# Steps of an attention stage spread over more rounds, with a gate's projection beside them; earlier copies of projections and a norm end in two parts

## The chip, the cores and the metric

The kernel runs on one core of a Trainium2 chip. The metric is the device time of one execution in microseconds (us); the time before is the median of three runs. The engines are TensorE (PE in the profile; PEld is its loading of weights), VectorE (DVE), ScalarE (ACT), GpSimd (POOL) and SyncE (SP), which here only starts transfers.

## The reference, cut to what matters

Three blocks follow one another on 512 tokens of width 1024, all in float32. The change touches two places.

The first is the even mixer of block one. Its input projection gives, among others, the queries, keys and values of a delta rule, a gate `z` (512 columns) that only scales the delta rule's output, and the queries, keys and values of a differential attention:

```python
qkv_a, z_a, b_a, a_a, q_b, k_b, v_b = split_cols(h @ w_in, EVEN_SPLITS)
o_a = gated_delta_rule(q_a, k_a, v_a, g, beta)
o_a = rms_norm(o_a, gdn_norm_w) * silu(z_a)
# differential attention: 4 heads, 4 blocks of 128 queries, causal
a = softmax(s0) - lam * softmax(s1)        # two score maps per head
o_b = a @ v_b
```

The second is the RWKV part of block three: eight pairs of heads run a delta rule with a per-channel decay over chunks of 64 tokens. Its inputs r, k, v are projections mixed with the token before (`out = (1-m)*t + m*shift(t)`), and its output goes through a group norm of 64 channels, gets a bonus term added and is multiplied by a gate `g` (a small matmul):

```python
y = group_norm(o) * gn_g + gn_b + bonus
y = y * g
```

## The kernel before, in words

Every engine has its own program, written out by Python; semaphores (`wait_ge`) join them. Activations are feature-major: a tile is 128 channels x 512 tokens. A projection (`Weights.tile`) of 128 output channels is 24 matmuls of 128x512: eight slices of the contraction, each in three products of a high and a low fp32r part. The weights come by SP's transfers into three raw buffers (two neighbouring tiles in one 1 MB transfer); ACT makes the high part (L87) and DVE the low part (L96), one tile ahead of the matmuls. `Weights.half` gives half a tile, 12 matmuls, and holds its PSUM bank in between. `Psum.take` hands out the eight banks in turn; before a bank is written again, PE waits for the engine that reads it out.

**Even mixer.** `Even.pe` orders the projections: 12 tiles `even.qkv`, 4 tiles `even.z`, one of 8 columns `even.ba`, 8 tiles `even.rope` with a rotation matmul each, then `even.dv`. When `even.ba` is done ACT copies it and then starts the transfer of the positions; from these DVE and ACT make the sine and cosine tables, and the copy of the first rope tile stands behind them on ACT. `z` goes through Silu as it is copied from PSUM. A fence of all engines follows, then the differential attention (`diff_*`), a fence, and the delta rule (`gdn_*`).

The attention has 16 units (head, query block `qt`). `waves(16, 4)` gives every engine the order: in round r the unit r-3 does its phase 3, unit r-2 phase 2, unit r-1 phase 1, unit r phase 0. Phase 0: PE makes two score maps (`diff.s`). Phase 1: DVE takes the masked maximum of each (L105), ACT the exponential with its sum (L84). Phase 2: DVE takes reciprocals (L108), scales and joins the two maps (L99, L102), PE transposes the result block by block (L93), and DVE (even units) or ACT (odd ones) copies it out (L87). Phase 3: PE multiplies with the values, and the other of the two engines copies the 128x128 result. Within phase 2 all of this is one chain.

**RWKV.** `Rwkv.steps` gives the orders. There are 16 units u (a pair of heads n = u//2, half of the tokens each), one started every six rounds; a unit's steps stand in the list `order`, one a round. Within a round an engine goes through the kinds of step in its own tuple (`PE`, `ACT`, `DVE`, `POOL`). Beside these run the projections of r, k, v of the next pair (kind `proj`, rounds 4 to 9 of each twelve, half a tile a round) and a convolution (`cf`: projections in rounds 0 to 3; `tap`: products on ACT, sums on POOL, and taps on DVE). When a second half is done ACT copies the projection twice (`shift_act`: into a padded buffer, L87, and scaled, L83), and that frees its bank; in `ACT` this stands behind the kinds `p` and `g`. Of kind `p`, step `pB` on ACT is a square root that waits for a matmul of the same round, a table load, and an exponential that waits for a scan on DVE (L3195). The group norm is `gn1` to `gn3`, an empty round, and `gn4`: there PE spreads the reciprocal roots (16 matmul instructions of 128x128 and 64 columns of weights) and makes the gate's matmul, and DVE does three operations of 128x512. ACT's next `out` waits for the last of them (`rw_gn`).

## Time and profile before

| | |
|---|---|
| median of three runs | 3913.9 us (3910.14 to 3914.62) |
| profiled execution | 3902.29 us, its span 3899.7 us |
| PE, DVE, ACT, POOL busy | 88%, 52%, 33%, 9% of the span |
| granted clock of TensorE, mean | 0.93 |
| matmuls of 128x512 fp32r | 10368, 2468.5 us busy |

Times are in us from the start of the span. A row of windows has the stretch, its length, then the busy time (and instructions) of PE, PEld, DVE, ACT and POOL, then PEclk, the DMA share and GB/s. In a timeline a row is a run of like instructions: start, duration, engine, line, operation, output and inputs, count, and in brackets the idle time before it and what ended it. PEclk is the granted clock as a share of 2.4 GHz, so that 0.50 is 1.2 GHz. Only the part up to 460 us (even mixer) and that from 2550 to 3250 us (RWKV) are touched.

### The profile page before, as it was taken

Reading aid. Unit: us, or ns where it says so; the run is one execution under the profiler, and the core shown is the slowest. Engines: PE = TensorE matmul, PEld = TensorE weight load, DVE = VectorE, ACT = ScalarE, POOL = GpSimd, SP = SyncE. Lnnn points to the kernel's source line nnn. Section 1 sums busy time; section 2 is a strip of 40 time slices with the busy share of each in tenths; the row PEclk is TensorE's granted clock in tenths of the full one; section 3 lists DMA queues with packets and bytes.
Section 4 is the critical chain, followed back from the end, with each engine's and each line's share of the span. In section 5 each row is a group of like instructions: output and inputs, shape, how many; then the busy total and the mean of one; then the engine's idle time right before and its main releaser. Section 6 shows DMA issues by size and latency. Waiting matters only on the chain.

```text
span 3899.7 us, 50586 instructions
## 1 busy us (share of the span) xinstructions
PE 3445.0 (88%) x20778; PEld 2657.7 (68%) x20778; DVE 2039.2 (52%) x3588; ACT 1295.9 (33%) x2133; POOL 366.1 (9%) x338
## 2 busy tenths in 40 slices
PE   6876889999799999998797889878989889998998
PEld 4645867777586677776666666456777777777886
DVE  5435446664422456654454435468676773445443
ACT  3222133222222332223333234355454542324221
POOL 0001200000000000000001000035443430000000
PEclk8976989999898999999897989889899989999999
DMA  3210013442343134432211120021111102232221
GB/s 132 66 43 1 1 60 108 135 141 87 60 88 74 33 92 130 137 107 87 79 52 42 47 80 12 27 87 45 32 38 41 48 13 76 71 114 86 91 94 64
DMA packets 318851, 274.89 MB, mean 70 GB/s; under 512 B 10912, under 2 KB 310048, under 8 KB 317856
## 3 DMA queue, kind: packets, MB, share of 16 engines
q1 hardware_dynamic: 314368, 256.07, 22.3%
q10 hardware_dynamic: 4256, 15.59, 1.1%
q8 instruction: 167, 2.74, 0.3%
q14 instruction: 60, 0.49, 0.0%
HBM read 265.35 MB, written 6.29 MB: 70 GB/s over the span
## 4 chain that ended last, share of the span: by engine, by line
PE 75%; DVE 14%; ACT 5%; issue 3%; DMA 1%; POOL 1%; DVEq 0%; ACTq 0%; SPq 0%; POOLq 0%
PE ps L90 73%; DVE f L102 5%; DVE f L96 3%; DVE r L96 3%; PE ps L93 2%; ACT f L83 2%; DVE f L99 2%; DVE f L108 1%; ACT r L87 1%; ACT f L87 1%; POOL f L96 1%; ACT L83 1%; ACT f L84 1%; DVE f L3195 0%; DVE f L105 0%
## 5 line engine op out<-in xcount | busy, mean ns | idle before, releaser
L90 PE MATMUL ps<-r,r 128*128 128x512 f32 x10368 | 2468.5, 397 | 143.5 <-DVE r L96 99.3
L90 PEld LDWEIGHTS ps<-r,r 128*128 128x128 f32 x10368 | 1931.9, 191 | 632.4 <-issue 193.6
L90 PE MATMUL ps<-f,f 64*64 64x64 f32 (+10 forms) x9458 | 909.0, 283 | 234.1 <-DVE f L96 58.9
L90 PEld LDWEIGHTS ps<-f,f 64*64 64x64 f32 (+4 forms) x9458 | 641.8, 162 | 485.3 <-issue 256.5
L96 DVE TENSOR_TENSOR r<-f,r 128x1024 fp32r<-128x1024 f32 (+2 forms) x619 | 654.3, 1063 | 491.7 <-ACT r L87 484.8
L87 ACT ACTIVATE r<-f 128x1024 fp32r<-128x1024 f32 (+2 forms) x548 | 507.1, 938 | 824.6 <-PE ps L90 679.7
L87 ACT ACTIVATE f<-ps 128x512 f32<-128x512 f32 (+3 forms) x414 | 184.6, 460 | 669.5 <-PE ps L90 424.7
L102 DVE SCALAR_TENSOR_TENSOR f<-f,f,f 128x128 f32<-128x128 f32 (+3 forms) x622 | 362.0, 588 | 41.6 <-ACT f L83 25.5
L96 POOL TENSOR_TENSOR f<-f,f 128x512 f32<-128x512 f32 (+2 forms) x280 | 322.1, 1164 | 514.5 <-ACT f L83 293.7
L96 DVE TENSOR_TENSOR f<-ps,f 128x512 f32<-128x512 f32 (+4 forms) x325 | 178.1, 561 | 327.7 <-PE ps L90 320.1
L83 ACT ACTIVATE f<-ps 128x512 f32<-128x512 f32 (+3 forms) x203 | 111.9, 553 | 636.3 <-PE ps L90 634.5
L96 DVE TENSOR_TENSOR f<-f,f 128x256 f32<-128x256 f32 (+5 forms) x372 | 220.8, 605 | 18.7 <-ACT f L83 10.1
L96 POOL TENSOR_TENSOR r<-f,r 128x512 fp32r<-128x512 f32 (+1 forms) x25 | 38.5, 1539 | 1985.4 <-ACT r L87 1985.4
L96 DVE TENSOR_TENSOR f<-f 128x512 f32<-128x512 f32 x129 | 86.9, 687 | 227.8 <-ACT f L83 216.5
L108 DVE RECIPROCAL f<-f 128x1 f32<-128x1 f32 (+4 forms) x193 | 72.3, 382 | 212.7 <-ACT f L84 106.1
L93 PE MATMUL ps<-f,f 128*128 128x128 f32 (+2 forms) x568 | 110.9, 316 | 63.3 <-DVE f L102 29.3
L83 ACT ACTIVATE f<-f 128x512 f32<-128x512 f32 (+8 forms) x206 | 100.3, 514 | 187.7 <-DVE f L102 86.1
L96 DVE TENSOR_TENSOR f<-f,ps 128x512 f32<-128x512 f32 (+1 forms) x192 | 110.7, 593 | 73.3 <-PE ps L90 62.7
L93 PEld LDWEIGHTS ps<-f,f 128*128 128x128 f32 (+2 forms) x568 | 73.4, 159 | 90.3 <-DVE f L102 34.0
L83 ACT ACT_TABLE_LOAD x90 | 115.5, 1283 | 32.1 <-DVE f L105 19.0
L83 ACT ACTIVATE f<-f,f 128x512 f32<-128x512 f32 (+2 forms) x165 | 109.5, 705 | 14.9 <-POOL f L96 13.9
L102 DVE SCALAR_TENSOR_TENSOR f<-ps,f,f 128x512 f32<-128x512 f32 x48 | 36.0, 751 | 146.2 <-PE ps L90 141.5
(32 smaller groups left out, 733.4 us busy)
## 6 DMA issues: line engine op xcount, KB each, us to landing
f<-in_w_mlp_up SPq DMA_DIRECT2D x32, 1024.0 KB, 6.5
f<-in_w_mlp_down SPq DMA_DIRECT2D x32, 1024.0 KB, 6.5
f<-in_w_ff SPq DMA_DIRECT2D x32, 1024.0 KB, 5.3
f<-in_w_ada SPq DMA_DIRECT2D x48, 512.0 KB, 4.1
f<-in_w_in SPq DMA_DIRECT2D x24, 1024.0 KB, 5.3
f<-in_w_in SPq DMA_DIRECT2D x44, 512.0 KB, 3.8
f<-in_w_in_even SPq DMA_DIRECT2D x12, 1024.0 KB, 6.0
f<-in_w_in_odd SPq DMA_DIRECT2D x12, 1024.0 KB, 13.1
```

Of the source, the lines that this page charges most:

```text
L83: return self.e.activation(out, in_, func, bias=bias, scale=scale)
L84: return self.e.activation(out, in_, func, bias=bias, scale=scale, accum_out=acc)
L87: return self.e.activation(out, in_, ACT.Copy) if self.name == "act" else self.e.tensor_copy(out, in_)
L90: return self.e.matmul(out, l, r, start=first, stop=last)
L93: return self.e.transpose(out, in_, ident)
L96: return self.e.tensor_tensor(out, a, b, op)
L99: return self.e.tensor_scalar(out, a, s1, None, o0) if o1 is None else self.e.tensor_scalar(out, a, s1, s2, o0, o1)
L102: return self.e.scalar_tensor_tensor(out=out, in0=a, scalar=s, in1=b, op0=o0, op1=o1)
L108: return self.e.reciprocal(out, in_)
```

## The change

In the even mixer the four tiles of `z` leave the projections. They become eight half tiles, one at the start of each of the attention's first eight rounds; ACT copies each finished tile without Silu, and four Silu of 128x512 stand behind the last round, before the fence. The unit's steps get a round each: transposes are phase 3, the product with the values phase 4, its copy phase 5. All copies of transposes go to ACT; the products of a head's four blocks gather in one held bank, copied once by ACT. DVE has maxima and the joining of the maps only, the maxima first in a round. In RWKV, ACT's kinds `cf` and `proj` are split: the steps of odd rounds (second halves, with their copies) come before `p` and `g`. The group norm's end is two steps: `gn4` (PE's spread and DVE's scaling) goes into the empty round, a round earlier, and `gn5` (the gate's matmul, the other two operations) stays.

```diff
@@ Even.pe
-        for n in range(4):
-            G.tile(pe, ("even.z", n), W, 1536 + n * 128, 128, X, [("ev_z", n + 1)])
@@ Even.diff_pe
-        for u, p in waves(16, 4):
+        K, G, X = self.K, self.K.G, self.norm.X
+        for u, p in waves(16, 6):
             if p == 0:
+                if u < 8:
+                    G.half(pe, ("even.z", u // 2), self.W, 1536 + u // 2 * 128, X, [("ev_z", u // 2 + 1)], u % 2)
                 for m in range(2):
...
-            elif p == 2:
+            elif p == 3:
                 pe.wait_ge("diff_a", u + 1)
-                b = self.bank["t", u] = K.ps.take(pe, ("diff_pt" + "da"[u % 2], u // 2 + 1))
+                b = self.bank["t", u] = K.ps.take(pe, ("diff_pt", u + 1))
...
-            elif p == 3:
-                pe.wait_ge("diff_pt" + "da"[u % 2], u // 2 + 1)
-                b = self.bank["o", u] = K.ps.take(pe, ("diff_o" + "ad"[u % 2], u // 2 + 1))
+            elif p == 4:
+                pe.wait_ge("diff_pt", u + 1)
+                if qt == 0:
+                    self.bank["o", h] = K.ps.hold(pe, ("diff_o", h + 1))
+                b = self.bank["o", h]
                 for kt in range(qt + 1):
...
@@ Even.act
-        for n in range(4):
-            G.act(act, ("even.z", n))
-            act.wait_ge("mm", K.done["even.z", n])
-            act.f(self.z[:, n, :], G.at["even.z", n], ACT.Silu).then_inc(S("ev_z"), 1)
@@ Even.diff_act
-        for u, p in waves(16, 4):
+        for u, p in waves(16, 6):
-            if p == 1:
+            if p == 0 and u < 8:
+                k = ("even.z", u // 2)
+                self.K.G.act(act, k)
+                if u % 2:
+                    act.wait_ge("mm", K.done[k])
+                    act.cp(self.z[:, u // 2, :], self.K.G.at[k]).then_inc(S("ev_z"), 1)
+            elif p == 1:
...
-            elif p == 2 and u % 2:
+            elif p == 3:
                 act.wait_ge("mm", K.done["diff.t", u])
...
-            elif p == 3 and not u % 2:
+            elif p == 5 and qt == 3:
                 act.wait_ge("mm", K.done["diff.o", u])
-                act.cp(self.o[:, 4 + h, qt * 128:km], K.ps.t[self.bank["o", u]][:, 0:128]).then_inc(S("diff_oa"), 1)
+                act.wait_ge("mm", K.done["even.z", 3])
+                act.cp(self.o[:, 4 + h, :], K.ps.t[self.bank["o", h]][:, :]).then_inc(S("diff_o"), 1)
+        act.wait_ge("ev_z", 4)
+        for n in range(4):
+            act.f(self.z[:, n, :], self.z[:, n, :], ACT.Silu).then_inc(S("ev_zs"), 1)
@@ Even.diff_dve
-        for u, p in waves(16, 4):
+        for u, p in ((r - p, p) for r in range(21) for p in (1, 2, 0) if 0 <= r - p < 16):
+            if p == 0 and u < 8:
+                K.G.dve(dve, ("even.z", u // 2))
-                if not u % 2:
-                    dve.wait_ge("mm", K.done["diff.t", u])
...
-                    dve.cp(self.pt[u % 3][:, 0:km], K.ps.t[self.bank["t", u]][:, 0:km]).then_inc(S("diff_ptd"), 1)
-            elif p == 3 and u % 2:
-                dve.wait_ge("mm", K.done["diff.o", u])
-                dve.cp(self.o[:, 4 + h, qt * 128:km], K.ps.t[self.bank["o", u]][:, 0:128]).then_inc(S("diff_od"), 1)
@@ Rwkv
-    ACT = ("out", "xy", "tm", "fin", "p", "g", "cf", "proj", "tap")
+    ACT = ("out", "xy", "tm", "fin", "cf1", "proj1", "p", "g", "cf", "proj", "tap")
@@ Rwkv.steps
-        order += ["fin", ("c", 0), ("c", 1), ("c", 2), ("c", 3), "out", "gn1", "gn2", "gn3", "", "gn4"]
+        order += ["fin", ("c", 0), ("c", 1), ("c", 2), ("c", 3), "out", "gn1", "gn2", "gn3", "gn4", "gn5"]
...
-                elif k == "proj":
-                    if r < 84 and 4 <= r % 12 < 10:
+                elif k in ("proj", "proj1"):
+                    if r < 84 and 4 <= r % 12 < 10 and (not split or r % 2 == (k == "proj1")):
@@ Rwkv.pe, after the spread of gn4
+            elif p == "gn5":
                 pe.wait_ge("rw_xg", 1)
                 b = self.bank["g3", n] = take(pe, ("rw_gn", n + 1))
                 K.mm_done(pe.mm(P[b][:, :], self.g2[:, ncol], self.xg, True, True), ("rw.g3", n))
@@ Rwkv.dve, after gn4's scaling by gn_g
+            elif p == "gn5":
                 dve.wait_ge("rw_ys", n + 1)
```

## Rows read from the trace of the kernel before

**Rows 1.** Windows: even projections, attention, and four RWKV periods; columns as told above.

```profile
37.00:266.60 229.60, 197.95 (x748) 138.77 (x748) 106.03 (x145) 64.01 (x87) 0.00 (x0) 0.92 0.22 66
266.60:350.30 83.70, 52.51 (x184) 31.07 (x184) 39.53 (x166) 25.29 (x82) 0.00 (x0) 0.56 0.00 0
2837.50:3168.00 330.50, 287.81 (x4151) 234.07 (x4148) 235.46 (x446) 163.46 (x294) 135.98 (x126) 0.92 0.13 38
```

**Rows 2.** Waits in the window 264:372 (us in total, times, longest).

```profile
ACT f L84 <- DVE f L105: 36.8, 9, 5.4
...
PE ps L93 <- DVE f L102: 29.3, 16, 3.4
```

**Rows 3.** Timeline of all engines, attention: table load, then a unit with `qt` 3.

```profile
267.48 1.28 ACT L83 ACT_TABLE_LOAD   x1 [18.97 <-DVE f L105]
268.77 0.20 ACT L83 ACTIVATE f<-f 128x2 f32<-128x2 f32 x1
...
281.95 0.68 DVE L105 CUSTOM_DVE_ANT_0 f<-ps,f 128x512 f32<-128x512 f32 x1
...
290.07 0.29 DVE L87 COPY f<-ps 128x128 f32<-128x128 f32 x1 [3.77 <-PE ps L90]
...
310.14 0.29 DVE L87 COPY f<-ps 128x128 f32<-128x128 f32 x1 [3.95 <-PE ps L90]
```

**Rows 4.** Timeline of PE alone, one RWKV period.

```profile
2947.81 0.68 PE L90 MATMUL ps<-f,f 64*64 64x64 f32 x16 [0.73 <-ACT f L83]
...
2956.10 2.02 PE L90 MATMUL ps<-f,f 64*64 64x64 f32 x32 [2.11 <-ACT f L83]
2958.06 5.00 PE L90 MATMUL ps<-r,r 128*128 128x512 f32 x12
...
2977.41 1.12 PE L90 MATMUL ps<-f,f 64*64 64x64 f32 x16 [3.86 <-issue]
2980.16 1.99 PE L90 MATMUL ps<-f,f 64*64 64x128 f32 x32 [1.62 <-issue]
...
3000.53 1.20 PE L90 MATMUL ps<-f,f 64*64 64x64 f32 x32 [1.21 <-ACT f L87]
3001.66 3.01 PE L90 MATMUL ps<-r,r 128*128 128x512 f32 x12
```

**Rows 5.** Timeline of PE alone, even projections.

```profile
38.05 13.92 PE L90 MATMUL ps<-r,r 128*128 128x512 f32 x48 [16.65 <-DVE r L96]
53.06 11.32 PE L90 MATMUL ps<-r,r 128*128 128x512 f32 x48 [1.10 <-DVE r L96]
...
114.27 33.23 PE L90 MATMUL ps<-r,r 128*128 128x512 f32 x144 [0.88 <-DVE r L96]
156.32 2.08 PE L90 MATMUL ps<-f,f 128*128 128x512 f32 x2 [8.83 <-ACT f L87]
```

**Rows 6.** The page's groups: DVE's part of the weight splits, among others.

```profile
L96 DVE TENSOR_TENSOR r<-f,r 128x1024 fp32r<-128x1024 f32 (+2 forms) x619 | 654.3, 1063 | 491.7 <-ACT r L87 484.8
```

**Rows 7.** Timeline of ACT alone, seventh round of that period.

```profile
2952.67 0.17 ACT L83 ACTIVATE f<-ps 128x4 f32<-128x4 f32 x1 [2.29 <-PE ps L90]
...
2955.37 0.68 ACT L83 ACTIVATE f<-ps,f 128x512 f32<-128x512 f32 x1
```

**Rows 8.** Windows: 3 us behind the gap that ends at 2956.10.

```profile
2956.00:2959.00 3.00, 2.90 (x34) 2.66 (x35) 2.44 (x6) 3.00 (x7) 2.12 (x2) 0.50 0.00 0
```

**Rows 9.** Timeline of PE alone: behind the same wait in another period, and a spread.

```profile
3042.36 3.92 PE L90 MATMUL ps<-r,r 128*128 128x512 f32 x12
...
3245.28 1.97 PE L90 MATMUL ps<-f,f 128*64 128x128 f32 x16 [0.59 <-DVE f L108]
```

**Rows 10.** Timeline of DVE alone, third, eighth and ninth round.

```profile
2927.11 1.22 DVE L96 TENSOR_TENSOR f<-f,f 128x256 f32<-128x256 f32 x3
...
2963.48 0.28 DVE L102 SCALAR_TENSOR_TENSOR f<-f,f,ps 128x64 f32<-128x64 f32 x1 [3.49 <-PE ps L90]
...
2969.98 3.24 DVE L96 TENSOR_TENSOR f<-f,f 128x256 f32<-128x256 f32 x3
2973.15 0.73 DVE L102 SCALAR_TENSOR_TENSOR f<-f,f,ps 128x512 f32<-128x512 f32 x1
```

More of the change, by code:

```diff
@@ L17 @@
 STAGES = (
-    {"ev_z": 4, "ev_pad": 12, "ev_padz": 3, "ev_conv": 12, "ev_qkv": 12, "ev_bar": 1, "ev_ba": 1, "ev_y": 1, "ev_na": 1,
-     "ev_beta": 1, "ev_rope": 8, "ev_dv": 4},
-    {"diff_elam": 1, "diff_exp": 32, "diff_oa": 8, "diff_pta": 8, "diff_lam": 2, "diff_max": 32, "diff_a": 16, "diff_ptd": 8,
-     "diff_od": 8},
+    {"ev_pad": 12, "ev_padz": 3, "ev_conv": 12, "ev_qkv": 12, "ev_bar": 1, "ev_ba": 1, "ev_y": 1, "ev_na": 1, "ev_beta": 1,
+     "ev_rope": 8, "ev_dv": 4},
+    {"diff_elam": 1, "diff_exp": 32, "ev_z": 4, "diff_pt": 16, "diff_o": 4, "ev_zs": 4, "diff_lam": 2, "diff_max": 32,
+     "diff_a": 16},
     {"gdn_expR": 4, "gdn_DTe": 4, "gdn_ekdf": 4, "gdn_ebE": 4, "gdn_y0": 12, "gdn_y1": 12, "gdn_NW": 4, "gdn_o": 4,
@@ L1006, in diff_pe @@
                 K.mm_done(t, ("diff.t", u))
-            elif p == 3:
-                pe.wait_ge("diff_pt" + "da"[u % 2], u // 2 + 1)
-                b = self.bank["o", u] = K.ps.take(pe, ("diff_o" + "ad"[u % 2], u // 2 + 1))
+            elif p == 4:
[3 more added lines that the diff above has]
+                b = self.bank["o", h]
                 for kt in range(qt + 1):
-                    t = pe.mm(K.ps.t[b][:, 0:128], self.dv[:, kt, h * 128:h * 128 + 128], self.pt[u % 3][:, kt * 128:kt * 128 + 128],
-                              kt == 0, kt == qt)
+                    t = pe.mm(K.ps.t[b][:, qs], self.dv[:, kt, h * 128:h * 128 + 128], self.pt[u % 3][:, kt * 128:kt * 128 + 128],
+                              qt + kt == 0, qt + kt == 6)
                 K.mm_done(t, ("diff.o", u))
+                if qt == 3:
+                    K.ps.leave(b)
     def gdn_pe(self, pe):
@@ L1148, in diff_act @@
                     act.wait_ge("mm", K.done["diff.o", u - 3])
-                act.cp(self.pt[u % 3][:, 0:km], K.ps.t[self.bank["t", u]][:, 0:km]).then_inc(S("diff_pta"), 1)
-            elif p == 3 and not u % 2:
+                act.cp(self.pt[u % 3][:, 0:km], K.ps.t[self.bank["t", u]][:, 0:km]).then_inc(S("diff_pt"), 1)
+            elif p == 5 and qt == 3:
                 act.wait_ge("mm", K.done["diff.o", u])
-                act.cp(self.o[:, 4 + h, qt * 128:km], K.ps.t[self.bank["o", u]][:, 0:128]).then_inc(S("diff_oa"), 1)
+                act.wait_ge("mm", K.done["even.z", 3])
[3 more added lines that the diff above has]
+            act.f(self.z[:, n, :], self.z[:, n, :], ACT.Silu).then_inc(S("ev_zs"), 1)
     def gdn_act(self, act):
@@ L1194, in dve @@
             t.then_inc(S("ev_conv"), 1)
-        for n in range(4):
-            G.dve(dve, ("even.z", n))
         G.dve(dve, "even.ba")
@@ L2875, in steps @@
         order = ["pA", "pB", "pC", "pD", "pE", "tm", "i0"] + [(k, l) for l in range(1, 6) for k in "yx"]
-        order += ["fin", ("c", 0), ("c", 1), ("c", 2), ("c", 3), "out", "gn1", "gn2", "gn3", "", "gn4"]
-        kind = {"x": "xy", "y": "xy", "gn1": "g", "gn2": "g", "gn3": "g", "gn4": "g"}
+        order += ["fin", ("c", 0), ("c", 1), ("c", 2), ("c", 3), "out", "gn1", "gn2", "gn3", "gn4", "gn5"]
+        kind = {"x": "xy", "y": "xy", "gn1": "g", "gn2": "g", "gn3": "g", "gn4": "g", "gn5": "g"}
+        split = "proj1" in kinds
         kind.update((k, "p") for k in order[0:5])
@@ L2886, in steps @@
             for k in kinds:
-                if k in ("cf", "tap"):
+                if k in ("cf", "cf1", "tap"):
                     for m, what, q in self.cf.steps(r - behind if k == "tap" else r):
-                        if (k == "tap") == (what in ("tap", "keep")):
+                        if (k == "tap") == (what in ("tap", "keep")) and (k == "tap" or not split or q == (k == "cf1")):
                             yield m, m, 0, "cf" + what, q
-                elif k == "proj":
-                    if r < 84 and 4 <= r % 12 < 10:
+                elif k in ("proj", "proj1"):
+                    if r < 84 and 4 <= r % 12 < 10 and (not split or r % 2 == (k == "proj1")):
                         n = r // 12 + 1
```

5 lines of the change are left out of this document (1 added, 4 removed).

## The prediction

> **What bounds the kernel now.** I read first the windows by stage. While the even projections run, PE is busy 198 of 230 us at a clock of 0.92, so whatever PE does there costs its full time; in the attention it is busy 52.5 of 83.7 us at 0.56, DVE 39.5 and ACT 25.3 [rows 1]. No engine is full there. The waits tell the rest: ACT stands 36.8 us for DVE's maxima and PE 29.3 us for DVE's joined maps [rows 2], a chain of one unit after another. In the timeline the same copy comes back after 20.07 us (290.07, 310.14) [rows 3]: four units take that, 5.02 each. In RWKV PE is busy 288 of 330 us, DVE 235, ACT 163, at 0.92 [rows 1]. That is near PE's limit, and what can be won is PE's idle time and what the low clock behind it costs. A period (twelve rounds, one pair of heads, a fourth of that window: 82.6 us) has five such gaps: 0.73, 2.11, 3.86, 1.62 and 1.21 us [rows 4].
>
> **Part 1a: `z` leaves the projections.** 144 matmuls (z, ba, the first rope tile) run without a break in 33.23 us [rows 5]; 96 of them are z: 22.2 us. Behind them PE waits 8.83 us for the first rope copy [rows 5]. That wait hangs on `even.ba` (copy, transfer of the positions, tables), and moves with it; nothing on it gets shorter. But ba's small weights are ready sooner than a full tile's, so of the gap of 0.88 us at 114.27 [rows 5] most goes too. Removed: 23.0 us (bounds 22.2 and 23.1). z's four Silu copies on ACT lay under PE's matmuls, so leaving them out is worth nothing there.
>
> **Part 1b: the attention.** I take the new stage in four pieces.
> Rounds 0 to 7: z's 96 matmuls, 22.2 us on PE. A start at the low clock costs 13.92 - 11.32 = 2.6 us more [rows 5]. Beside it PE has 8 units' scores, 5 of transposes and 4 of products, about 1.35 heads of the 4. The stage's 52.5 us at 0.56 [rows 1] are 52.5 x 0.56 / 4 = 7.35 us a head at full clock, so 9.9. Sum 34.7, or 4.3 a round. What else runs is hidden under that: DVE's 39.5 us [rows 1] less its sixteen copies (about 5.7) are 2.1 a unit, and a weight split of some 1.1 [rows 6] every second round; ACT has less. The first unit's wait for lambda goes under z as well. The two 1 MB weight transfers move behind those of `even.dv`, on SP's queue alone; the DMA share in this stage is 0.00 [rows 1], so they are hidden, and `even.out`'s, now behind them, are needed only after the delta rule. If not hidden, the first would be late by a few us.
> Rounds 8 to 15: every step now stands a round from the next. DVE's 2.1 us a unit are 2.4 with gaps; PE has 52.5 / 16 = 3.3 at about the low clock, 1.8 at the full. Which of them holds depends on the clock, so I take 2.7, nearer DVE, the engine that the waits name: 21.6 (bounds 19.2 and 26.4).
> Drain of the last unit: as now from the first maximum to the last copy, 281.95 to 290.36, 8.4 us [rows 3].
> The four Silu at the end are covered by nothing, since the fence waits for them: a table load of 1.28 us [rows 3] and four times 0.6, the present copies' time, 3.7 us.
> Sum 68.4 against 83.7: 15.3 saved. The delta rule's first Exp now needs a table load too, in front of work that DVE waits for: 1.3 lost (0 if it runs while PE is still at work).
> The Trainium skill (ScalarE: Activation LUTs, "What ACT_TABLE_LOAD costs") speaks against this edit: it puts each switch of table set at about 2.66 us, drain included. In the trace the load is 1.28 us and the activation behind it starts 0.01 us later [rows 3]; by the Trainium skill's figure the two switches would cost 5.3 us in place of 2.6, and the saving would be 2.7 less.
> Part 1: 23.0 + 15.3 - 1.3 = 37.0 us (bounds 31 and 40).
>
> **Part 2: RWKV.** Following `take` and `hold` through a period shows whose bank PE waits for.
> (a) In the eighth round the second `x` step takes the bank of the projection whose copies stand behind ACT's `pB`. ACT's root waits 2.29 us for PE until 2952.67; the scaled copy begins only at 2955.37 [rows 7], and when it ends PE resumes, at 2956.10 [rows 4]. Put in front, both copies (1.2 us) fit into the 2.29 and delay the root by nothing or little. PE gets back 2.1 us, and more: behind the gap the clock is 0.50 [rows 8], the twelve matmuls take 5.00 us in place of 3.01, the 32 small ones 2.02 in place of 1.20 [rows 4]. That makes 4.9 us in three periods and 3.6 in two (3.92 in place of 3.01 [rows 9], the small ones in proportion), and 3.4 in an earlier one: 25.3. Against it, PE's spread of `gn4` now stands before the end of this round: 1.97 us at the low clock [rows 9], 1.0 at the full, five times. Net 20.3.
> (b) In the second round it is the convolution's bank: 1.21 us [rows 4], five times, 6.0.
> (c) The 0.73 us of the seventh round [rows 4] wait for the norm's root behind DVE's shifted sum, which is late by ACT's copy; I take half, as PE's own matmul then comes last: 2.0 in all.
> (d) The 3.86 us [rows 4] wait for DVE, which in the ninth and tenth round does product, norm end, shift and `x` without a pause. One of these, 0.73 us [rows 10], moves a round forward, where DVE stands idle for 3.49 us [rows 10]: 3.7 in five periods. The 1.62 us behind it stay.
> Sum 32.0. Against this, POOL's masks stand behind the convolution's sums, and PE will now ask for them some 3 us sooner; I take off 6.0, a little over 1 us a period, as an estimate without a row. Part 2: 26 us (bounds 0 and 36).
>
> **Sum.** 63 us. The profiled execution took 3902.3 us, 2.6 of them around its span, and would take 3839.3; the median of the runs shown is 11.6 us above it, so I predict 3913.9 - 63 = 3851 us.
>
> **Rivals.**
> R1: the freed bank only shows the next wait. DVE's ninth round and POOL's masks set the period, and RWKV gives 8 in place of 26: 3869. For it: DVE has 235 of 330 us of work [rows 1], and the longest gap is already its own. Against: DVE itself waits 3.49 us for PE in the eighth round [rows 10].
> R2: the clock stays low in the attention. z's matmuls take twice their time, 22 us more: 3873. For it: the stage is at 0.56 now [rows 1]. Against: the same matmuls one behind the other lose only 2.6 us at a cold start [rows 5].
> R3, the other side: DVE's operations on two SBUF operands are slower beside POOL's sums; three of 128x256 take 3.24 us in one round and 1.22 in another [rows 10], 0.67 us more for each. If the closer packing brings 19 more of them a period under POOL, a period grows by 12.7 us and five of them by 63, and from there on the kernel is slower; with 25 it takes 3935. For it: that row. Against: POOL is busy 136 of 330 us [rows 1], and the overlap can as well shrink.
> The Trainium skill (SBUF — State Buffer, "Who interferes with whom") has this as a lock: such an operation and one of GpSimd that reads SBUF exclude each other. By that rule the trace agrees, as 1.08 us for an operation of 0.41 is a wait and not a slower rate alone.
>
> **How the numbers follow.** Chances: forecast 0.66, R1 0.16, R2 0.11, R3 0.03, no gain in either part 0.04. What a measurement of this kernel can tell from no change is 0.2%, 7.8 us. The forecast's own range is 3838 (both parts at their upper bounds) to 3864; with R1 and R2 and a little of both together it is 3835 to 3881. From the same cases: faster 0.93, same 0.04, slower 0.03.
>
> **What would show it.** Right: no z between qkv and ba, and the attention starting 23 us sooner; the attention in 66 to 72 us, with the clock near 1 in its first half, DVE almost without waits in its second, and a table load with four activations behind the last copy; in RWKV no PE wait of 2.1 or 1.2 us on L83 or L87, the full clock in the eighth round, a period of 77 to 78 us. Wrong: z halves of 5 us, rounds over 5 us, or a new PE wait on POOL or DVE in rounds eight to eleven.

## The result and the profile after

| | before | after |
|---|---|---|
| timed runs, median | 3912.1 us (3910.1 to 3914.6, 4 runs) | 3821.7 us (3820.8 to 3823.2, 4 runs) |
| profiled execution, span | 3899.7 us | 3819.4 us |
| mean granted clock of PE | 0.930 | 0.943 |

The ratio of the runs is 0.9769, with a 95% interval of 0.9752 to 0.9786: the kernel is 2.3% faster. Forecast were 3851 us and a range of 3835 to 3881, so the direction was right and the time is 13 us below the range. The gain is 90.4 us by the medians and 80.3 us by the two traces; 63 were forecast.

GpSimd's memsets mark the borders of stages. These are the rows of after, from the timeline of POOL alone: the first is the start of the delta rule, the second the stage behind it, `128x1` the start of the RWKV blocks, and each `128x64` one pair of heads.

```profile
307.20 0.52 POOL L114 MEMSET f<- 128x512 f32 x1 [269.56 <-ACTq L76]
1010.93 2.30 POOL L114 MEMSET f<- 128x160 f32 x5
2509.94 0.25 POOL L114 MEMSET f<- 128x1 f32 x4 [72.55 <-DMA x_rest<-f]
...
3128.26 0.15 POOL L114 MEMSET f<- 128x64 f32 x1
```

In before the same rows stand at 350.48, 1053.64, 2552.38 and 3207.96. So after is 43.3 us ahead at the delta rule, 42.4 at the start of the RWKV blocks and 79.7 at their end. Two places gave everything: what lies ahead of the delta rule, and the RWKV blocks (655.6 us before, 618.3 after: 37.3).

The windows of after, which answer to [rows 1]: even projections, attention, and two RWKV periods.

```profile
core 0: us, PE busy (x) PEld busy (x) DVE busy (x) ACT busy (x) POOL busy (x), PEclk, DMA share, GB/s
37.00:243.70 206.70, 175.25 (x652) 120.29 (x652) 101.94 (x141) 58.55 (x80) 0.64 (x4) 0.91 0.21 63
243.70:307.20 63.50, 54.01 (x280) 37.23 (x281) 38.87 (x154) 37.66 (x99) 0.00 (x0) 0.96 0.11 34
2861.84:2938.88 77.04, 71.23 (x1039) 57.83 (x1036) 60.72 (x112) 41.71 (x75) 35.78 (x32) 0.93 0.13 39
2938.88:3015.51 76.63, 70.46 (x1038) 57.15 (x1036) 60.67 (x112) 41.57 (x75) 35.71 (x32) 0.96 0.13 40
```

In the attention PE now carries 96 more matmuls and is busy for nearly the same time as before, 54.0 against 52.5 us, because its clock is 0.96 and no longer 0.56. The stage is 63.5 us long instead of 83.7. A finer cut shows its two halves, with z and without:

```profile
243.70:278.86 35.16, 35.11 (x163) 24.86 (x163) 18.68 (x69) 17.82 (x44) 0.00 (x0) 0.95 0.19 61
278.86:296.20 17.34, 15.08 (x93) 9.40 (x92) 16.53 (x73) 12.70 (x42) 0.00 (x0) 1.00 0.00 1
281.20:289.84 8.64, 7.51 (x46) 4.70 (x46) 8.23 (x37) 6.45 (x21) 0.00 (x0) 1.00 0.00 1
```

With z, PE is busy 35.1 of 35.2 us: it is the bound. Without z a round takes 8.64 / 4 = 2.16 us, and DVE (8.23 of 8.64) is the fullest engine, PE (7.51) close behind. The end of the stage, from the last copy on, and the delta rule's load, on ACT alone:

```profile
302.87 0.60 ACT L87 ACTIVATE f<-ps 128x512 f32<-128x512 f32 x1 [1.25 <-PE ps L90]
303.48 1.28 ACT L83 ACT_TABLE_LOAD   x1
304.78 2.19 ACT L83 ACTIVATE f<-f 128x512 f32<-128x512 f32 x4
309.78 1.28 ACT L83 ACT_TABLE_LOAD   x1 [2.82 <-PE ps L90]
```

In RWKV, PE's waits from the first marker to the last, first of before (655.6 us), then of after (618.3 us); columns: total, times, longest.

```profile
PE ps L90 <- issue: 45.7, 19, 8.1
PE ps L90 <- ACT f L83: 20.6, 12, 4.7
...
PE ps L90 <- ACT f L87: 6.5, 6, 1.2
```

```profile
PE ps L90 <- issue: 44.5, 18, 7.2
...
PE ps L90 <- ACT f L83: 4.7, 1, 4.7
PE ps L90 <- ACT f L87: 2.1, 5, 0.7
```

What PE waited for on ACT went from 27.1 to 6.8 us, 20.3 us; nothing else moved by more than 1.2. PE's busy time fell too, with the same 7651 matmuls, from 564.1 to 548.3 us: 15.7 us, which I put down to the low clock behind those waits (it is 548.4 us too where ACT's order alone is changed, below). 20.3 + 15.7 + 1.3 make the 37.3. The timeline of PE in a period of after, beside [rows 4]:

```profile
2971.17 3.02 PE L90 MATMUL ps<-r,r 128*128 128x512 f32 x12
...
2977.11 3.06 PE L90 MATMUL ps<-r,r 128*128 128x512 f32 x12
...
2988.64 1.12 PE L90 MATMUL ps<-f,f 64*64 64x64 f32 x16 [3.94 <-issue]
2991.38 1.98 PE L90 MATMUL ps<-f,f 64*64 64x128 f32 x32 [1.62 <-issue]
...
2996.37 1.40 PE L90 MATMUL ps<-f,f 64*64 64x64 f32 x40 [0.36 <-ACT f L87]
```

The twelve matmuls of the eighth round take 3.02 us in place of 5.00, and of the period's five gaps two are left, those behind DVE, of the same size as before. One wait behind ACT's L87 remains, of 0.36 us.

### The profile page after: what moved, and what is told of

Its sections match the earlier page's. It is cut to its first block, busy times and chain, and to the rows that moved or that the text cites. A ratio compares the mean times of both kernels' runs of the same rounds, so it can differ in the third digit from the quotient of the medians.

```text
span 3819.4 us, 50585 instructions
## 1 busy us (share of the span) xinstructions
PE 3408.5 (89%) x20778; PEld 2633.2 (69%) x20778; DVE 2047.8 (54%) x3572; ACT 1304.7 (34%) x2143; POOL 374.7 (10%) x338
## 4 chain that ended last, share of the span: by engine, by line
PE 77%; DVE 12%; ACT 5%; issue 3%; DMA 1%; POOL 1%; DVEq 0%; ACTq 0%; SPq 0%; POOLq 0%
PE ps L90 75%; DVE f L102 4%; DVE f L96 3%; DVE r L96 3%; PE ps L93 2%; ACT f L83 2%; DVE f L108 1%; DVE f L99 1%; ACT r L87 1%; ACT L83 1%; POOL f L96 1%; ACT f L87 1%; DVE f L105 0%; ACT f L84 0%; DMA f<-in_w_in_odd 0%
## 5 line engine op out<-in xcount | busy, mean ns | idle before, releaser
L90 PE MATMUL ps<-f,f 64*64 64x64 f32 (+11 forms) x9458 | 885.9, 278 | 215.3 <-DVE f L96 59.0
L90 PEld LDWEIGHTS ps<-f,f 64*64 64x64 f32 (+4 forms) x9458 | 626.5, 159 | 458.5 <-issue 254.8
L87 ACT ACTIVATE r<-f 128x1024 fp32r<-128x1024 f32 (+2 forms) x548 | 507.1, 938 | 825.7 <-PE ps L90 681.0
L87 ACT ACTIVATE f<-ps 128x512 f32<-128x512 f32 (+3 forms) x422 | 189.5, 465 | 668.7 <-PE ps L90 416.6
L96 POOL TENSOR_TENSOR f<-f,f 128x512 f32<-128x512 f32 (+2 forms) x280 | 330.7, 1194 | 469.7 <-ACT f L83 256.9
L93 PE MATMUL ps<-f,f 128*128 128x128 f32 (+2 forms) x568 | 106.5, 307 | 36.7 <-DVE f L99 19.0
```

The lines of the kernel that those rows point to most:

```text
L87: return self.e.activation(out, in_, ACT.Copy) if self.name == "act" else self.e.tensor_copy(out, in_)
L90: return self.e.matmul(out, l, r, start=first, stop=last)
L93: return self.e.transpose(out, in_, ident)
L96: return self.e.tensor_tensor(out, a, b, op)
```

## The experiments

Four columns are taken from the memsets of each trace: the time to the start of the delta rule; the delta rule (from there to the `128x160` memset); and the RWKV blocks (`128x1` to the last `128x64`). What lies between is 1498 to 1502 us in all traces but one. Medians of different experiments compare only roughly: the kernel after itself gave 3821.7 us in one session and 3833.3 in another. So what an edit is worth is read below from the stages of the traces.

| kernel | timed median, us | ratio to before [95%] | to delta rule | delta rule | RWKV |
|---|---|---|---|---|---|
| before | 3912.1 | 1 | 350.5 | 703.2 | 655.6 |
| after | 3821.7 | 0.9769 [0.9752, 0.9786] | 307.2 | 703.7 | 618.3 |
| attention only | 3866.4 | 0.9898 [0.9878, 0.9918] | 307.0 | 704.0 | 655.6 |
| RWKV only | 3871.6 | 0.9912 [0.9897, 0.9927] | 353.6 | 706.6 | 619.9 |
| ACT's order only | 3869.6 | 0.9907 [0.9892, 0.9922] | 351.6 | 707.0 | 619.6 |
| norm split only | 3908.3 | 1.0003 [0.9993, 1.0013] | 352.4 | 707.6 | 655.8 |
| z back | 3831.2 | 0.9805 [0.9791, 0.9820] | 311.6 | 705.2 | 618.4 |
| Silu later | 3820.7 | 0.9782 [0.9766, 0.9798] | 303.3 | 704.1 | 618.3 |
| sums moved | 3828.6 | 0.9793 [0.9771, 0.9816] | 309.8 | 709.4 | 614.4 |
| both of these | 3818.9 | 0.9774 [0.9759, 0.9788] | 307.0 | 705.2 | 614.3 |
| steps adjacent | 3847.1 | 0.9845 [0.9831, 0.9860] | 326.1 | 708.4 | 618.3 |
| projections first | 3883.2 | 0.9935 [0.9919, 0.9952] | 351.6 | 708.1 | 627.9 |
| convolution first | 3890.9 | 0.9959 [0.9944, 0.9974] | 350.9 | 703.2 | 642.3 |
| both, first block as it was | 3817.9 | 0.9771 [0.9757, 0.9784] | 303.8 | 703.8 | 617.2 |
| after again | 3833.3 | 0.9812 [0.9798, 0.9825] | 308.3 | 704.1 | 621.0 |
| before again | 3908.0, one run | | 352.5 | 707.5 | 655.5 |

Each ratio is against runs of before on the same chip; their medians were 3905.7 to 3907.8 us in these experiments.

**The two parts apart.** Each part alone, put into the kernel before. For the attention:

```diff
+        for u, p in waves(16, 6):
+            if p == 0 and u < 8: G.half(pe, ("even.z", u // 2), ...)
...
     ACT = ("out", "xy", "tm", "fin", "p", "g", "cf", "proj", "tap")    # as before
```

> The kernel before with the whole first part (z's projections inside the attention, its steps a round apart, one bank of outputs for a head, Silu behind it) and none of the changes to the RWKV blocks. My theory: the two parts do not meet, so this gives what the marker at the start of the delta rule moved between the two traces, 43.3 us, less the 0.8 us that the delta rule gave back: about -42.5 us, 0.989 of the time before. The attention stretch takes 63 to 64 us against 83.7. Rival A: part of the 90 us is a shift of the whole program (the median of before stood 10 us above its profiled execution, the median of after did not), so this kernel's timed runs gain 10 us more than its trace shows. Rival B: the RWKV blocks lose clock or place when they start earlier: less than 38 us are gained.

Measured: -41.4 us by the medians, -43.0 by the spans (3856.7). The attention's window is the same as in after, 63.5 us at a clock of 0.96.

> The kernel before with all changes to the RWKV blocks' order (early copies on ScalarE, the norm's end in two steps) and none to the attention. My theory: 37.9 us, as the stretch of the RWKV blocks shrank between the two traces, 0.990 of the time before; this and the run with the attention's part alone add up to the whole change within 2 us by their traces. Rival: the 10 us between the profiled execution and the timed runs of before belong to one of the two parts; then one of these two kernels gains 48 to 53 us in its timed runs.

Measured: -36.2 us by the medians; the RWKV blocks shrink by 35.7 us. The medians of the two add up to 77.6 us, the stages of the two traces to 43.5 + 35.7 = 79.2, beside 80.3 for the whole. So the parts add up, and neither hides 10 us. The trace of the second kernel has one surprise: the stages ahead of RWKV, whose code is that of before, are 6.8 us longer than in the trace of before. That is taken up below.

**Which edit of the RWKV part does it.**

```diff
-    ACT = ("out", "xy", "tm", "fin", "p", "g", "cf", "proj", "tap")
+    ACT = ("out", "xy", "tm", "fin", "cf1", "proj1", "p", "g", "cf", "proj", "tap")
```

> The kernel before with ScalarE's new order alone: its copies of projections and convolution results for a pair's odd rounds go ahead of the steps p and g; the norm's end is not split. My theory: PE's waits for a bank in the eighth round (12 gaps of about 5 us in the trace of before, one in each pair) and the low clock behind them are ScalarE's lateness, so this alone gives most of the 37.9 us: the gap of 5.00 goes and the clock stays at its upper level in the eighth round, 2.1 us of each pair, and with it the 0.73 and 2.1 gaps ahead of it: -24 us or so, 20 to 30. Rival: the 5 us gap is set by VectorE's gn4 step behind it as much as by ScalarE (both free the same bank's neighbours), and the order alone gives under 12 us.

The other edit alone:

```diff
-        order += [..., "gn1", "gn2", "gn3", "", "gn4"]
+        order += [..., "gn1", "gn2", "gn3", "gn4", "gn5"]
...
+            elif p == "gn5":
```

> The kernel before with the norm's end split alone: gs and its product in one round, g3 and what follows it one round later; ScalarE's order is as before. My theory: PE does not wait for gs and g3 of one round together, but its bank waits in the eighth round stay, since ScalarE still copies late: between 3 and 14 us faster (the 37.9 us less what the order alone gives). Rival: splitting alone makes the pipeline one round deeper with nothing gained where ScalarE is late: within 3 us of before, or slower.

ACT's order alone brings RWKV to 619.6 us, as far as both edits together (619.9): 36.0 us, over the 20 to 30 that I expected. That expectation also misread a row: the 5.00 us of [rows 4] are the duration of twelve matmuls at the low clock and no gap, and the wait ahead of them is the 2.11. The split of the norm's end alone leaves RWKV at 655.8. It is worth nothing in either company. The eighth round, in the timeline of PE, of the kernel with the split alone:

```profile
2962.28 2.02 PE L90 MATMUL ps<-f,f 64*64 64x64 f32 x32 [2.09 <-ACT f L83]
2964.23 4.94 PE L90 MATMUL ps<-r,r 128*128 128x512 f32 x12
...
2983.58 1.12 PE L90 MATMUL ps<-f,f 64*64 64x64 f32 x16 [3.94 <-issue]
```

and with ACT's order alone:

```profile
3024.27 3.02 PE L90 MATMUL ps<-r,r 128*128 128x512 f32 x12
...
3027.99 2.16 PE L90 MATMUL ps<-f,f 64*64 64x64 f32 x36 [0.45 <-DVE f L102]
...
3036.86 1.12 PE L90 MATMUL ps<-f,f 64*64 64x64 f32 x16 [3.43 <-issue]
```

With the split the gap behind DVE is 3.94 us, without it 0.45 + 3.43. The DVE work that the split takes forward returns its wait elsewhere. The other half of my expectation, 3 to 14 us from the split, was wrong.

**Which copies of ACT.** ACT's new order cut in two: only the projections' copies first, or only the convolution's.

```diff
-    ACT = (..., "fin", "p", "g", "cf", "proj", "tap")
+    ACT = (..., "fin", "proj1", "p", "g", "cf", "proj", "tap")     # one kernel
+    ACT = (..., "fin", "cf1", "p", "g", "cf", "proj", "tap")       # the other
```

> The kernel before with only one half of ScalarE's new order: its copies of the projections' odd rounds (5, 7 and 9 of a pair's twelve) go ahead of the steps p and g, those of the convolution's inputs stay behind. My theory: TensorE's wait of 5 us and the lower clock in the eighth round, and the 2.1 us gap ahead of it, are for banks that projection copies free; this half gives most of the order's 36 to 38 us, 25 to 35. Rival: the convolution's copies (rounds 1 and 3) are the late ones, and this half gives under 10 us.

> The kernel before with only the other half: ScalarE's copies of the convolution's inputs in rounds 1 and 3 of a pair go ahead of p and g, the projections' copies stay behind. My theory: this half gives the rest, 2 to 10 us (the gap of 1.21 us in the first rounds of a pair, and what it hides). Rival: it gives over 20 us.

RWKV shrinks by 27.7 us with the projections' copies first and by 13.3 with the convolution's first; 36.0 with both. In the timeline of PE of the second, the eighth round's wait is still there, but the clock behind it is back sooner:

```profile
2950.96 1.20 PE L90 MATMUL ps<-f,f 64*64 64x64 f32 x32 [2.07 <-ACT f L83]
2952.08 4.62 PE L90 MATMUL ps<-r,r 128*128 128x512 f32 x12
```

The 32 small matmuls take 1.20 us where before took 2.02 [rows 4], at the same wait ahead of them. In this period that is 0.8 us, and 0.4 at the twelve behind them, 1.2 beside the 1.21 of the gap that goes. The convolution's half was over my 2 to 10 us. The two halves alone add up to 41.0 us and give 36.0 together, so they share 5.0. Most of that is clock: PE's busy time in RWKV falls by 12.4 us with the one, by 6.7 with the other and by 15.7 with both.

**What distance and z do in the attention.** The steps of a unit next to each other again, in the kernel after:

```diff
-        for u, p in waves(16, 6):
+        for u, p in waves(16, 4):
...
-            elif p == 3:        # transpose; ACT's copy of it likewise
+            elif p == 2:
-            elif p == 4:        # product
+            elif p == 3:
...
-        for u, p in ((r - p, p) for r in range(21) for p in (1, 2, 0) if 0 <= r - p < 16):
+        for u, p in ((r - p, p) for r in range(19) for p in (2, 1, 0) if 0 <= r - p < 16):
```

> The kernel after with the attention's steps for a unit put back next to each other: TensorE transposes two rounds behind the scores and multiplies three rounds behind (not three and four), ScalarE copies the transposed tile in the same round as TensorE makes it, and VectorE takes its steps in the old order. One bank of outputs for a head, ScalarE doing all copies and z inside stay. My theory: a round again holds a chain VectorE, TensorE, ScalarE, TensorE of one unit, which in the trace of before made a round of 4 to 5 us out of engines that have 2 to 3 us of work; the eight rounds with z hide part of it (+0.5 us each), the eight without go from 2.2 to about 4 us: 15 to 20 us slower than after, with the lower clock of TensorE (0.56 in before) coming back in the second half. Rival: the gain comes from ScalarE doing all copies and from the output bank held for a head (fewer copies, fewer waits for a bank), and distance adds little: under 6 us slower.

Measured: the attention takes 18.9 us longer. (The delta rule takes 4.6 us longer too, but a kernel with the attention of after, the one with the sums moved, has 709.4 us there, so that this is not shown to come from the steps.) The window of the attention, and then one wait in the part without z, from the timeline of PE:

```profile
243.70:326.05 82.35, 62.94 (x280) 42.08 (x280) 39.38 (x152) 37.67 (x99) 0.00 (x1) 0.83 0.08 26
```

```profile
287.93 1.12 PE L93 MATMUL ps<-f,f 128*128 128x128 f32 x4 [2.16 <-DVE f L102]
```

PE waits for DVE's joined maps as before, and the stage's clock falls from 0.96 to 0.83, so that the same 280 matmuls keep PE busy for 62.9 us and not 54.0. So the distance between the steps is worth much, and the rival's "under 6 us" is wrong. The edit moves the steps of PE and of ACT and DVE's order within a round at once; which of the three counts for how much was not separated. The stage is nearly as long as the old one, 82.4 and 83.7 us, but with z's matmuls in it, and so distance is not all. In the half without z, DVE's joining of a full map, in the timeline of DVE alone:

```profile
302.06 0.75 DVE L102 SCALAR_TENSOR_TENSOR f<-f,f,f 128x512 f32<-128x512 f32 x1
316.99 0.75 DVE L102 SCALAR_TENSOR_TENSOR f<-f,f,f 128x512 f32<-128x512 f32 x1
```

Four units take 14.9 us here, 20.1 in before [rows 3] and 8.6 in after: 3.7, 5.0 and 2.2 each. Of the 2.9 us a unit gained, distance gives 1.6. The other 1.3 come with what this kernel shares with after: ACT's copies, the held bank and the higher clock that z's half leaves behind (0.79 from 278.8 to 318.0 us, 0.56 in the old stage). Which of them is not shown.

z's projections and their Silu back where they were, with the new steps:

```diff
+        for n in range(4):
+            G.tile(pe, ("even.z", n), W, 1536 + n * 128, 128, X, [("ev_z", n + 1)])
...
-                if u < 8:
-                    G.half(pe, ("even.z", u // 2), ...)
```

> The kernel after with z's four projections and their Silu back among the even projections; the attention keeps its new steps, a round apart. My theory: the two edits of the first part are worth about 22.9 us (z out of the projections) against its price inside the attention. Back in the projections z costs 22.9 us again; the attention's first eight rounds fall from 4.3 to the 2.2 us of the rounds without z (about -17 us), and Silu with its table load leaves the end (-3.5 us), and the delta rule's table load goes (-1.3 us). So +1 to +3 us against after: moving z is worth next to nothing in itself, and the new steps alone carry the 42 us. Rival A: TensorE works through the attention at its upper clock because z's matmuls fill it; without them the clock falls back to its lower level in the attention (0.56 in the trace of before) and in the delta rule behind it, and the kernel is 10 to 20 us slower than after. Rival B: z's rounds are longer than 2.2 us by less than z's work, and the kernel is over 5 us slower than after with the clock high.

Measured in the trace: 5.8 us more than after where RWKV starts. The attention is 45.0 us long, at a clock of 0.77:

```profile
266.60:311.60 45.00, 36.94 (x184) 23.46 (x183) 33.63 (x150) 27.63 (x86) 0.00 (x0) 0.77 0.00 1
```

z costs 22.9 us in the projections and 18.5 us in the attention, its Silu included: 4.4 us of gain. Another 1.5 us lie in the delta rule, which is within what its length varies by (below). My +1 to +3 us were too low. Rival A had the mechanism, the clock does fall, but not its 10 to 20 us; Rival B had the size and not its high clock. So of the 42.4 us that after is ahead at the start of RWKV, 36.7 are there without moving z.

Of the 43.3 us by which the delta rule starts sooner, the distance accounts for 18.9 (the run before this one) and moving z for 4.4, each taken out of the full kernel. The 20.0 that remain belong to no edit that was isolated. Either ACT's copies and the held bank are worth that (sixteen times the 1.3 us above are 21, an estimate), or distance and z are worth more apart than on top of each other, since both use the idle time that PE had in the old attention, 31.2 of 83.7 us [rows 1]. Before with the new copies and the held bank alone was not run.

**The work at the attention's end.** The four Silu go into rounds of the delta rule's last chunk:

```diff
-        act.wait_ge("ev_z", 4)
-        for n in range(4):
-            act.f(self.z[:, n, :], self.z[:, n, :], ACT.Silu).then_inc(S("ev_zs"), 1)
...
+                if c == 3 and p in (4, 6, 8, 10):
+                    z = self.z[:, p // 2 - 2, :]
+                    act.f(z, z, ACT.Silu).then_inc(S("ev_zs"), 1)
```

> The kernel after with the four Silu of z moved from the attention's end into rounds of the delta rule's last chunk, where ScalarE is idle. My theory: behind the attention's last copy everything waits for ScalarE: a table load of 1.28 us, four Silu of 2.19 us, and the delta rule's first Exp loads its table again, 1.28 us; all three leave the path, 3.5 + 1.3 = 4.8 us, and the loads come back in the last chunk, where up to 2.6 us of them could show if ScalarE is needed there. So -3 to -5 us against after. Rival: the delta rule's start is held by PE and VectorE work that goes on beside these, and nothing is gained (within 1 us).

The delta rule starts 3.9 us sooner, 3.6 to 4.0 us are kept at the later markers, and 3.2 by the spans. Of the 3.9, 0.4 lie ahead of the attention's last copy. From the start of that copy to the start of the delta rule it is 4.33 us in after and 0.83 here: 3.5 us, which is the four Silu (2.19 us) and the table load (1.28 us). All three traces with this edit have 0.83 or 0.84 us there. In the kernel with both edits the delta rule nevertheless starts at 307.0 us: its attention starts 0.8 us later than that of after, and the clock is 0.65 in its last 11 us and not 0.91. The Trainium skill (ScalarE: Activation LUTs, "What ACT_TABLE_LOAD costs") puts a switch at about 2.66 us, which would make it 4.9 us for the switch and the four Silu, an estimate; the trace does not agree, neither with its 3.5 us nor with the rows at 303.48 and 309.78 above, where each load is 1.28 us. What the second load, inside the delta rule, costs is not seen: that stage takes 704.1 us without it and 703.7 with it.

**DVE beside GpSimd.** GpSimd's sums leave the ninth and tenth round and follow two steps later:

```diff
     def products(self, t):
-        return range(2 * t, min(2 * t + 2, self.more))
+        s = t if t < 3 else t - 2
+        return range(2 * s, min(2 * s + 2, self.more)) if t not in (3, 4) else range(0)
```

> The kernel after with the sums that GpSimd adds up in an RWKV pair taken out of the two rounds in which VectorE has its long operations (3.25 us each, three in a row, beside GpSimd's five of 8.19 us) and put one or two rounds later. My theory: VectorE's operations are stretched by GpSimd's while both work on SBUF (the same form takes 1.22 us elsewhere), and VectorE is what the one long gap of PE left in a period waits for (3.94 us, in the tenth round): the three operations fall to about 1.2 us and the gap with them, 3 to 4 us in each of five to six pairs, -15 to -20 us. Rival: GpSimd then stretches other work of VectorE in the rounds that it moves to by as much, and the time is within 3 us of after or above it.

> Both at once: Silu in the delta rule's last chunk and GpSimd's sums in later rounds. My theory: they touch different stages and add up, -18 to -25 us against after. Rival: as for each of them alone; then it is no better than the better one of the two.

The tenth round in after, DVE, then POOL:

```profile
2981.99 3.25 DVE L96 TENSOR_TENSOR f<-f,f 128x256 f32<-128x256 f32 x3
```

```profile
2982.06 2.88 POOL L96 TENSOR_TENSOR f<-f,f 128x512 f32<-128x512 f32 x2 [1.90 <-ACT f L83]
```

and the same with both edits, DVE, then PE:

```profile
2979.13 1.22 DVE L96 TENSOR_TENSOR f<-f,f 128x256 f32<-128x256 f32 x3
```

```profile
2983.75 0.68 PE L90 MATMUL ps<-f,f 64*64 64x64 f32 x16 [1.92 <-issue]
2986.49 1.98 PE L90 MATMUL ps<-f,f 64*64 64x128 f32 x32 [2.06 <-issue]
```

With POOL silent the three operations take 1.22 us and no longer 3.25, and PE's gap is 1.92 and no longer 3.94. The mechanism is shown. The gain is not what I expected: RWKV takes 3.9 us less, not 15 to 20. Of the 2.0 us in the tenth round 0.4 come back in the next gap, which grows from 1.62 to 2.06. Over RWKV PE's idle time falls by 6.7 us with both edits, and its busy time grows by 2.7, from 548.3 to 551.0, at the same number of matmuls. The four middle periods are 0.1 to 1.3 us shorter each. The periods at either end can't be compared by the memsets, which are GpSimd's own work and have moved with its order. The stretch up to the first memset of a pair, in after and then with both edits:

```profile
2509.94:2637.23 127.29, 101.41 (x769) 80.59 (x770) 93.51 (x109) 76.61 (x118) 62.66 (x50) 0.91 0.23 65
```

```profile
2511.04:2642.44 131.40, 108.42 (x842) 85.78 (x842) 99.19 (x115) 77.84 (x120) 64.06 (x50) 0.92 0.23 67
```

It is 4.1 us longer, but PE has 842 matmuls behind it and not 769. The two edits together came to 3818.9 us, not the 18 to 25 us below after.

The version with both edits and the first block's sums left in their old place, then after and before once more, on one chip:

> The kernel after with the four Silu in the delta rule's last chunk, and GpSimd's sums out of the two rounds in which they stretch VectorE, except in the first block, where moving them cost 4.1 us ahead of the first pair. My theory: 3.9 us from Silu, and in the RWKV blocks the 8 us that the run with both showed behind its first pair: -10 to -12 us against after on the same chip, 0.997 of its time. Rival: in the timed runs it is lost in what the clock does between runs (5 us either way), and the difference to after is under 5 us.

> The kernel after once more, beside the others on one chip. My theory: 3820 to 3826 us, 0.978 of before; in its trace the delta rule's first 450 to 700 us take the same as in the first trace of after, within 2 us.

> The kernel before once more, one profile. My theory: its executions come in two kinds, which differ at the start of the delta rule: after an attention at the lower clock TensorE either has the upper clock back 10 us into the delta rule (0.93 in the trace that was shown) or is at 0.58 to 0.68 there, and the 700 us from its start end 4 to 5 us later; the latter is the more frequent, so this profile should have a span of 3903 to 3908 us with its excess between the attention's start and the delta rule's first 100 us. Rival: the excess lies anywhere, in the later stages as much as here.

The first gives 3817.9 us (3816.9 to 3818.9), after in the same rounds 3833.3 (3826.1 to 3835.7): 15.5 us less, and 7.6 less by the spans (3816.3, 3823.9). It has the lowest median here, but the kernel with both edits is 1.0 us above it with runs from 3814.9 to 3821.2, so which of the two is faster is not shown. And after, repeated, is 11.6 us slower than in its first runs; against those the gain is 3.9 us. The 3.8 us ahead of the first pair did not come back, and need not: the memset has moved here too (842 matmuls ahead of it). My expectation took its -8 us for RWKV from that misreading. Against the first trace of after RWKV takes 1.1 us less, where with both edits everywhere it took 4.0 less.

**Where executions of one kernel differ.** The repeat of before has a span of 3905.5 us. Its memsets:

```profile
352.52 0.52 POOL L114 MEMSET f<- 128x512 f32 x1 [314.48 <-DVEq L76]
1060.04 2.30 POOL L114 MEMSET f<- 128x160 f32 x5
3213.79 0.15 POOL L114 MEMSET f<- 128x64 f32 x1
```

Against the first trace that is +2.0, +6.4 and +5.8 us: the difference arises ahead of the delta rule's end and stays the same behind it. The window from 10 us behind the start of the delta rule, first of the trace shown ahead of the prediction, then of the repeat:

```profile
360.00:370.00 10.00, 6.94 (x51) 5.96 (x51) 3.84 (x7) 1.19 (x2) 5.36 (x5) 0.93 0.00 0
```

```profile
362.00:372.00 10.00, 6.86 (x30) 6.20 (x31) 3.11 (x6) 0.60 (x1) 4.32 (x4) 0.60 0.00 0
```

The same program has the upper clock back in one and is near 1.2 GHz in the other, and gets 51 or 30 matmuls done. Of seven traces with the old attention two have 0.93 there and a delta rule of 703.2 us, five have 0.58 to 0.66 and 706.6 to 708.1. The new attention is not free of it: the kernel with the sums moved has 0.50 in that window and 709.4 us. The window alone does not tell the length, though: the kernel with Silu later has 0.66 there and 704.1 us. Later borders do the same. After a stretch with an idle PE, windows of 20 us in after, and aligned with them in the kernel with the sums moved:

```profile
1210.00:1230.00 20.00, 19.42 (x77) 12.59 (x77) 7.93 (x29) 6.31 (x19) 0.00 (x0) 0.75 0.00 1
1230.00:1250.00 20.00, 18.91 (x93) 11.44 (x92) 10.01 (x36) 7.78 (x25) 0.00 (x0) 1.00 0.00 1
```

```profile
1218.30:1238.30 20.00, 19.42 (x65) 11.71 (x64) 7.72 (x27) 5.09 (x17) 0.00 (x0) 0.67 0.00 1
1238.30:1258.30 20.00, 19.45 (x80) 11.27 (x79) 8.29 (x30) 6.73 (x21) 0.00 (x0) 0.85 0.00 1
```

That kernel loses 5.7 us between the end of its delta rule and the start of RWKV, in code that is the same in both. The repeat of after has one such place more: 130.1 us up to the first pair of heads in place of 127.3, with the same 769 matmuls, at a clock of 0.88 and not 0.91. The timed runs have no trace, so that their 12 us are of this kind is likely and not shown; for it speaks their mean clock, 0.942 or 0.943 in the first four runs of after and 0.939 or 0.940 in four of the five later ones.

## Why the prediction missed

In short: the mechanisms held, and terms of the sum did not. Too large was the time of the attention's rounds without z (21.6 us forecast, 17.3 measured); the discount of 6.0 us in RWKV had nothing behind it; the convolution's copies (6.0 forecast, 8.3 measured) were too small, as the clock behind the gap was left out. The scatter of the timed runs added some 10 us.

**The base.** I took the 11.6 us between the profiled execution and the median of before as fixed, part of any run. They are not. The profiled execution was one of the less frequent short ones; the repeat stands 5.7 us above it. The medians give 90.4 us in one comparison and 74.3 in the other (3907.6 to 3833.3), the traces 80.3 and 81.6. So of the 27 us by which I was off, about 17 are in the kernel and 10 in the scatter of the timed runs. A gain of 81 us from 3913.9 would be 3833, still 2 below the range. Both parts of the sum came out above their own upper bounds, 42.4 against 40 and 37.3 against 36. The other end of the forecast's own range, 3864, does not follow from its bounds: 31 and 0 would give 3883.

**Part 1a, right.** Forecast -23.0, measured -22.9: the attention starts at 243.7 and not at 266.6.

**Part 1b, rounds 0 to 7, right.** Forecast 34.7, measured 35.2. The first twelve matmuls of z took 4.58 us and the next 3.0: the cold start costs 1.6 us and not the 2.6 taken.

**Part 1b, rounds 8 to 15, mis-sized.** Forecast 21.6 with bounds of 19.2 and 26.4; measured 17.3. The step that failed is 2.7 us a round, "nearer DVE". DVE does bound it, but with 8.23 us for four units, 2.06 each, and with hardly a gap; my 2.4 for it "with gaps" was already too long, and so was the lower bound. PE's 1.8 at the full clock was right (7.51 / 4 = 1.88).

**Drain and Silu, right.** Forecast 8.4 + 3.7 = 12.1, measured 307.2 - 296.2 = 11.0. The delta rule's table load: 1.3 forecast; the stage is 0.6 longer (703.7 against 703.2), and, as said, no shorter where the load is gone, so no run shows the term. Part 1 in all: -37.0 forecast, -42.4 measured.

**Part 2, (a) and (c), right in the sum.** The wait behind ACT and the low clock behind it were put at 25.3 and 2.0, the projections' copies alone give 27.7. What failed is the subtraction, 5 us for PE's spread at the end of the eighth round: with ACT's order alone, where nothing moves there, RWKV takes as long as with both. Since (d) below, 3.7 the other way, failed as well, the two together put the sum off by only 1.3 us, which is luck.

**(b), mis-sized.** Forecast 6.0, the gap alone; measured 8.3 on top of the projections' half and 13.3 by itself. I took the gap alone, and none of the clock in the later rounds that comes back with it: 1.2 us in the period above.

**(d), wrong.** Forecast -3.7 from moving a DVE operation forward. The split of the norm's end is worth nothing, alone or with ACT's order, and the gap stays at 3.94 us.

**The discount, wrong.** 6.0 us were taken off, "an estimate without a row", for GpSimd's masks coming late. In the timeline of POOL the masks are not late, POOL waits for DVE ahead of them. It did so in before already, where the row could have been read; first before, then after:

```profile
2983.55 1.82 POOL L96 TENSOR_TENSOR f<-f,f 128x256 f32<-128x256 f32 x3 [4.11 <-DVE f L96]
```

```profile
2994.77 1.82 POOL L96 TENSOR_TENSOR f<-f,f 128x256 f32<-128x256 f32 x3 [4.11 <-DVE f L96]
```

Without it Part 2 would have been 32.0, and 37.3 were measured. The sum then is 69 us, and 3845. Of the 11.3 us by which Part 2 was too low, 6.0 are this discount, 2.3 (b), 1.3 the spread and (d) together and 0.4 (a) and (c); 1.3 lie between the traces of the order alone (36.0) and of after, and were not followed.

**The rivals.** R1 fell: the four middle periods are 76.6 to 77.2 us, close to the forecast (77 to 78), though its mechanism, DVE as the next wait, is what is left in the tenth round. R2 fell: the clock is 0.96. R3 fell: the three operations take 3.25 us as before (3.24) and DVE's busy time grew by 15 us over RWKV, 3 a period in place of the rival's 12.7, without becoming the bound. Its mechanism is real, and GpSimd's sums out of the way prove it: 1.22 us. The Trainium skill (SBUF — State Buffer, "Who interferes with whom") has this as a lock between such an operation and one of GpSimd that reads SBUF; by that rule the trace agrees.

## What to carry to other kernels

When a chain of engines sets the length of a stage, put each step a whole round behind the one that feeds it, in the order of every engine: here that distance was worth 18.9 us of a stage of 82.4. Undo each edit of a bundle in turn: distance and z, undone one by one, explain 18.9 and 4.4 of 43.3 us, and 20.0 stay with edits that no run isolates. When PE waits for a bank, look for the engine that frees it and at what stands ahead of that copy in its order; short copies moved forward gave 36 us, and of the whole part's 37.3 the clock behind the waits was 15.7. A marker that belongs to the engine whose order is changed moves with it: count the matmuls ahead of it. A discount without a row is worth no more than its row, and a base of one profiled execution carries its own luck: ask which stages of it might have had the clock by chance.

## What the runs showed of the hardware

How soon TensorE has its upper clock back behind a slack stretch differs between executions of the same program: 0.93 or 0.60 in the same 10 us of the delta rule, which takes 703.2 us in the one and 707.5 in the other; over the seven traces with the old attention it is 3.4 to 4.9 us longer at the lower clock. A table load of ScalarE is 1.28 us, with the next activation 0.02 us behind it at the attention's end, and the copy ahead of it ends 0.01 us before it starts; nothing more is seen of it. DVE's operation on two SBUF operands beside GpSimd's takes 1.08 us in place of 0.41.
